# One-core hybrid encoder step: the triangular inverse and the gated scores on packed 32 by 32 tiles

## What is computed

```python
# gated delta rule, per chunk and head
M = where(strict, beta * rel * (k @ k.T), 0)
sol = triangular_solve(eye + M, rhs)            # the kernel forms the inverse itself
# HGRN2, per chunk and head
A[t, s] = sum_d q[t, d] * k[s, d] * exp(G[t, d] - G[s, d])   for s <= t
```

## Time and profile before

| | |
|---|---|
| runs, median (lowest to highest) | 1079.43 us (1077.76 to 1082.05), 3 runs |
| profiled execution, its own time | 1077.1 us |
| its span in the trace | 1075.3 us |
| PE busy, PEld busy | 1043.8 us, 1006.2 us |
| DVE busy, ACT busy | 506.8 us, 381.1 us |
| mean granted clock of TensorE | 0.995 of full |

### The profile page before, as it was taken

The page is one execution under the profiler, slowest core; times in us unless marked ns, Lnnn a source line. Parts: engine busy times, 40 slices in busy tenths (PEclk is TensorE's granted clock), DMA queues, the critical chain, the costliest instruction groups (busy, mean ns, idle before and its releaser), DMA issues.

```text
span 1075.3 us, 20690 instructions
## 1 busy us (share of the span) xinstructions
PE 1043.8 (97%) x8773; PEld 1006.2 (94%) x8773; DVE 506.8 (47%) x910; ACT 381.1 (35%) x663; POOL 17.3 (2%) x28
## 2 busy tenths in 40 slices
PE   6999999999999999999999999999999999999997
PEld 5888998899999999999999999999999999999996
DVE  3569435442224654744743475444444444343432
ACT  6675344523432234236333323232322232212222
POOL 0000000000001000000000000000000000000000
PEclk9999999999999999999999999999999999999999
DMA  9922223430333244243263323223233232322212
GB/s 325 275 62 60 60 79 79 108 86 2 99 83 111 79 109 127 75 118 99 89 172 88 100 79 92 86 78 88 87 88 88 78 97 79 89 84 80 88 55 84
DMA packets 181749, 104.95 MB, mean 98 GB/s; under 512 B 4578, under 2 KB 179144, under 8 KB 181676
## 3 DMA queue, kind: packets, MB, share of 16 engines
q1 hardware_dynamic: 179484, 96.74, 31.6%
q0 software_dynamic: 1568, 4.90, 1.6%
q10 hardware_dynamic: 624, 2.23, 0.6%
HBM read 100.55 MB, written 3.31 MB: 97 GB/s over the span
## 4 chain that ended last, share of the span: by engine, by line
PE 89%; DVE 3%; ACT 3%; SPq 3%; issue 1%; DMA 1%; ACTq 0%; DVEq 0%
PE G L1670 70%; PE R L1678 15%; PE R L1681 2%; SPq L783 2%; PE G L1708 1%; DVE cy L1369 1%; DMA raw<-in_w_in 1%; ACT Um L943 1%; ACT w_hi L906 0%; DVE w_lo L1210 0%; DVE kPG L1439 0%; ACT X L943 0%; DVE kD L1441 0%; SPq L785 0%; DVE relT L1412 0%
## 5 line engine op out<-in xcount | busy, mean ns | idle before, releaser
L1670 PE MATMUL G<-h_hi,w_hi 128*128 128x272 f32 (+1 forms) x1456 | 428.5, 294 | 1.0 <-DVE w_lo L1210 0.8
L1670 PE MATMUL G<-h_lo,w_hi 128*128 128x272 f32 (+1 forms) x1456 | 422.0, 290 | 0.0
L1670 PE MATMUL G<-h_hi,w_lo 128*128 128x272 f32 (+1 forms) x1456 | 421.6, 290 | 0.0
L1670 PEld LDWEIGHTS G<-h_hi,w_hi 128*128 128x128 f32 x1456 | 276.0, 190 | 3.2 <-issue 1.4
L1670 PEld LDWEIGHTS G<-h_lo,w_hi 128*128 128x128 f32 x1456 | 276.4, 190 | 0.0
L1670 PEld LDWEIGHTS G<-h_hi,w_lo 128*128 128x128 f32 x1456 | 276.0, 190 | 0.0
L1210 DVE TENSOR_TENSOR w_lo<-raw,w_hi 128x1024 fp32r<-128x1024 f32 (+2 forms) x138 | 158.4, 1147 | 244.8 <-ACT w_hi L906 244.6
L906 ACT ACTIVATE w_hi<-raw 128x1024 fp32r<-128x1024 f32 (+2 forms) x138 | 136.4, 988 | 104.4 <-PE G L1670 90.3
L1670 PE MATMUL G<-a_hi,w_hi 128*128 128x272 f32 (+2 forms) x340 | 98.4, 290 | 0.4 <-DVE w_lo L1210 0.4
L1670 PE MATMUL G<-a_hi,w_lo 128*128 128x272 f32 (+2 forms) x340 | 98.2, 289 | 0.0
L1670 PE MATMUL G<-a_lo,w_hi 128*128 128x272 f32 (+2 forms) x340 | 97.9, 288 | 0.0
(11 more groups left out here) (250 smaller groups left out, 1349.2 us busy)
## 6 DMA issues: line engine op xcount, KB each, us to landing
raw<-in_w_in SPq DMA_DIRECT2D x48, 512.0 KB, 5.9
raw<-in_w_up SPq DMA_DIRECT2D x44, 512.0 KB, 3.8
raw<-in_w_ada SPq DMA_DIRECT2D x32, 512.0 KB, 4.6
wada<-in_w_ada SPq DMA_DIRECT2D x8, 1024.0 KB, 11.1
raw<-in_w_down SPq DMA_DIRECT2D x16, 512.0 KB, 3.9
raw<-in_w_out SPq DMA_DIRECT2D x8, 512.0 KB, 4.0
raw<-in_w_down SPq DMA_DIRECT2D x8, 384.0 KB, 3.4
xtok<-in_x_prompt ACTq DMA_DIRECT2D x4, 512.0 KB, 5.7
```

What stands on the lines that cost most here:

```text
L1670: ins = pe.matmul(out, w, x, start=(job.first and k == 0 and p == 0), stop=(job.last and k == job.nk - 1 and p == 2))
```

## The change

What the diff does:

- **Inverse, levels 0 to 4.** Only 32 by 32 blocks on the diagonal matter there. T, its transpose and X live in packed tiles Tc, Uc, Xc of 128 partitions by 10 times 32 columns. A step of `g_x`, `g_t` or `g_y` is 34 products of 32 by 32: 4 chunks times 2 heads times 4 diagonal blocks, and 2 for the sample. Block j stands on partitions 32j to 32j+31 for operands and result. All 34 go into one fill of one bank. The transposes of `g_t` and of `g_x` at level 0 become products with the identity (`turned`).
- **Inverse, levels 5 and 6.** Level 5: `g_x` is 16 products of 32 by 32, `g_y` is two fills of 8 and 16 products. Level 6: 8 products of 64 by 64 each for `g_x` and `g_y`. `g_t` of level 5 goes away. The results are assembled in Um (block copies on ACT and DVE) and in T64.
- **Scores.** `h_diag` and `h_level` 0 to 4: 34 products that contract 128 channels into 32 by 32 results, result block j on partitions 32j to 32j+31; level 5: 16 such, level 6: 8 of 64 by 64. DVE copies under the mask into a packed tile Sc; after level 4 ACT copies its blocks to N or PT, and DVE copies the blocks of levels 5 and 6 there directly.
- **Reads.** Each level's result is read by one instruction of 128 partitions by 256 columns and one of 32 by 64.
- **Constants.** The masks on the chip shrink to 32 columns per level; POOL clears T64 and Um, the second after a wait for the evacuation of the group "gagb".
- **Plan.** NEED changes in four places, so that the jobs fall a little otherwise between the steps.

```diff
+PACK = 2 * N_CHUNK
+LAST_SMALL = 4
...
-    NEED = dict(g_gram=3.0, g_tok=4.0, g_x=0.9, g_y=0.9, g_t=0.2, g_w=1.0, g_u=1.2, g_o=1.6, h_diag=2.2, h_level=2.4, h_k=2.5,
+    NEED = dict(g_gram=3.0, g_tok=4.0, g_x=0.8, g_y=1.0, g_t=0.2, g_w=1.0, g_u=1.2, g_o=1.6, h_diag=2.2, h_level=2.4, h_k=2.5,
                 h_o=1.4, g_norm=0.6, onorm=0.4)
     def need(step):
         name = step[0]
         if name == "g_x" and step[2] == 0:
-            return 2.6
+            return 1.5
         if name == "g_y" and step[2] == LEVELS - 1:
-            return 3.4
+            return 1.6
...
+            if 0 < lv <= LAST_SMALL + 1:
+                s.append(("g_t", pair, lv - 1))
             if lv:
-                s.append(("g_t", pair, lv - 1))
                 s.append(("g_y", pair, lv))
...
-        "g_x": ["dve" if name == "g_x" and a[1] == 0 else "act"] * short,
-        "g_y": ["dve"] * short, "g_t": ["act"] * short,
+        "g_x": ["dve" if name == "g_x" and a[1] == 0 else "act"],
+        "g_y": ["dve", "act"] if name == "g_y" and a[1] == LAST_SMALL + 1 else ["dve"], "g_t": ["act"],
...
-        masks = sb("masks", [P, LEVELS + 1, P])
+        masks = sb("masks", [P, 1, P])
+        masks_c = sb("masks_c", [P, LAST_SMALL + 2, QUAD])
+        Sc = sb("Sc", [P, PACK + 2, QUAD])
...
-        Tm = at("rec", "Tm", [P, CHUNKS, 2, P], off=base + 2 * tile)
+        Tc = at("rec", "Tc", [P, PACK + 2, QUAD], off=base + 2 * tile)
+        Uc = at("rec", "Uc", [P, PACK + 2, QUAD], off=base + 2 * tile + (PACK + 2) * QUAD * 4)
+        T64 = at("rec", "T64", [P, PACK, P // 2], off=base + 2 * tile + 2 * (PACK + 2) * QUAD * 4)
         Um = at("rec", "Um", [P, CHUNKS, 2, P])
-        X = at("rec", "X", [P, CHUNKS, 2, P])
-        Wn = X
-        masks_t = at("rec", "masks_t", [P, LEVELS, P])
+        Wn = at("rec", "Wn", [P, CHUNKS, 2, P])
+        Xc = at("rec", "Xc", [P, PACK + 2, QUAD], off=where["rec"] - tile)
+        X5 = at("rec", "X5", [P, PACK, QUAD], off=where["rec"] - tile + (PACK + 2) * QUAD * 4)
+        X6 = at("rec", "X6", [P, PACK, P // 2], off=where["rec"] - tile + (2 * PACK + 2) * QUAD * 4)
+        masks_t = at("rec", "masks_t", [P, LAST_SMALL + 1, QUAD])
         cols_neg = at("rec", "cols_neg", [P, CHUNKS, NH])
...
+        def packed(b):
+            return R[:, b, 0:PACK * QUAD].rearrange("p (m t) -> p m t", m=PACK)
+        def packed_sample(b):
+            return R[0:DEC, b, PACK * QUAD:(PACK + 2) * QUAD].rearrange("p (h t) -> p h t", h=2)
+        def quad(j):
+            return slice(j * QUAD, (j + 1) * QUAD)
+        def block_of(x, r, c):
+            return x[quad(r), 0:N_CHUNK, :, quad(c)].rearrange("p c h t -> p (c h) t")
+        def corner_of(x):
+            return x[0:P // 2, 0:N_CHUNK, :, P // 2:P].rearrange("p c h t -> p (c h) t")
+        def corner(b):
+            return R[0:P // 2, b, 0:PACK * P // 2].rearrange("p (m t) -> p m t", m=PACK)
...
-            sp.dma_start(masks[:, 0:LEVELS, :], t["level_masks"][:, 0:LEVELS, :]).then_inc(const_in, 16)
+            sp.dma_start(masks_c[:, :, :], t["level_masks_c"]).then_inc(const_in, 16)
...
+                pool.dma_start(Tc[:, 0:PACK, :], mid(t["unit_c"], PACK)).then_inc(Tc_unit, 16)
+                pool.dma_start(Tc[0:DEC, PACK:PACK + 2, :], mid(t["unit_c"][0:DEC], 2)).then_inc(Tc_unit, 16)
...
+                    pool.memset(T64[0:P // 2, :, :], 0.0).then_inc(inverse_zero, 1)
+                    wait_group(pool, groups_at["gagb", 0])
+                    pool.memset(Um[:, :, :, :], 0.0).then_inc(inverse_zero, 1)
...
+            def read_packed(n, dst):
+                act.wait_ge(fill_done, first_fill[n] + 1)
+                b = first_fill[n] % 4
+                act.activation(dst[:, 0:PACK, :], packed(b), ACT.Copy)
+                act.activation(dst[0:DEC, PACK:PACK + 2, :], packed_sample(b), ACT.Copy).then_inc(bank_user["act"], 1)
...
-                elif name == "g_x" and a[1]:
-                    read_banks(n, 0, chunk_pieces(X, True)[:len(bank_users(step))])
+                elif name == "g_x" and 0 < a[1] <= LAST_SMALL:
+                    read_packed(n, Xc)
+                elif name == "g_x" and a[1] == LAST_SMALL + 1:
+                    read_banks(n, 0, [(X5[:, :, :], packed)])
+                elif name == "g_x" and a[1] == LEVELS - 1:
+                    read_banks(n, 0, [(X6[P // 2:P, :, :], lambda b: R[P // 2:P, b, 0:PACK * P // 2]
+                                       .rearrange("p (m t) -> p m t", m=PACK))])
                 elif name == "g_t":
-                    read_banks(n, 0, chunk_pieces(Um, True)[:len(bank_users(step))])
+                    read_packed(n, Uc)
+                    if a[1] == LAST_SMALL:
+                        act.wait_ge(inverse_zero, 2)
+                        wait_bank(act, first_fill[n])
+                        for j in range(4):
+                            act.activation(block_of(Um, j, j), Uc[quad(j), 0:PACK, :], ACT.Copy)
+                        act.activation(Um[0:DEC, N_CHUNK, :, 0:DEC], Uc[0:DEC, PACK:PACK + 2, :], ACT.Copy)
+                elif name == "g_y" and a[1] == LAST_SMALL + 1:
+                    act.wait_ge(fill_done, first_fill[n] + 2)
+                    b = (first_fill[n] + 1) % 4
+                    for r, c in ((0, 1), (2, 3)):
+                        ins = act.activation(block_of(Um, r, c), packed(b)[quad(r)], ACT.Copy)
+                    ins.then_inc(bank_user["act"], 1)
...
+                elif name == "h_level" and a[1] == LAST_SMALL:
+                    act.wait_ge(at_zero, a[0] + 1)
+                    wait_bank(act, first_fill[n])
+                    for j in range(4):
+                        act.activation(block_of(scores(a[0]), j, j), Sc[quad(j), 0:PACK, :], ACT.Copy)
+                    act.activation(scores(a[0])[0:DEC, N_CHUNK, :, 0:DEC], Sc[0:DEC, PACK:PACK + 2, :], ACT.Copy)
...
+            def copy_packed(n, dst, mask, lv):
+                b = bank(n, 0)
+                dve.copy_predicated(dst[:, 0:PACK, :], mid(mask[:, lv, :].bitcast(U32), PACK), packed(b))
+                read(dve.copy_predicated(dst[0:DEC, PACK:PACK + 2, :], mid(mask[0:DEC, lv, :].bitcast(U32), 2),
+                                         packed_sample(b)))
...
-                    if lv < LEVELS - 1:
-                        copy_masked(n, Tm, masks_t, lv)
+                    if lv <= LAST_SMALL:
+                        copy_packed(n, Tc, masks_t, lv)
+                        if lv == LAST_SMALL:
+                            dve.wait_ge(inverse_zero, 2)
+                            wait_bank(dve, first_fill[n])
+                            for j in range(2):
+                                dve.tensor_copy(T64[quad(j), :, quad(j)], Tc[quad(j), 0:PACK, :])
+                    elif lv == LAST_SMALL + 1:
+                        read(dve.tensor_copy(T64[quad(1), :, quad(0)], packed(bank(n, 0))[quad(1)]))
                     else:
-                        wait_bank(dve, last_bank[spot("g_t", pair, lv - 1)])
-                        copy_masked(n, Um, masks, lv)
+                        read(dve.tensor_copy(corner_of(Um), corner(bank(n, 0))))
...
+                    link(dve.memset(Sc[:, :, :], 0.0))
+                    copy_packed(n, Sc, masks_c, LAST_SMALL + 1)
...
+                    if lv <= LAST_SMALL:
+                        copy_packed(n, Sc, masks_c, lv)
+                    elif lv == LAST_SMALL + 1:
+                        b = bank(n, 0)
+                        for r, c in ((0, 1), (2, 3)):
+                            ins = dve.tensor_copy(block_of(scores(pair), r, c), packed(b)[quad(r)])
+                        read(ins)
+                    else:
+                        read(dve.tensor_copy(corner_of(scores(pair)), corner(bank(n, 0))))
...
+            def quads(lhsT, rhs):
+                return [mm(lambda b, m=2 * c + h, j=j: packed(b)[quad(j), m, :], lhsT(c, h, j), rhs(c, h, j))
+                        for c in range(N_CHUNK) for h in range(2) for j in range(4)] + \
+                       [mm(lambda b, h=h: packed_sample(b)[:, h, :], lhsT(N_CHUNK, h, 0), rhs(N_CHUNK, h, 0))
+                        for h in range(2)]
+            def turned(block):
+                return quads(block, lambda c, h, j: ident[quad(j), quad(j)])
...
+                    if lv == 0:
+                        for k in range(len(FILLS)):
+                            wait_bank(pe, first_fill[spot("g_gram", pair)] + k)
+                        fill(n, 0, turned(lambda c, h, j: N[quad(j), c, h, quad(j)]))
+                    elif lv <= LAST_SMALL:
+                        wait_bank(pe, first_fill[spot("g_y", pair, lv - 1) if lv > 1 else spot("g_x", pair, 0)])
+                        fill(n, 0, quads(lambda c, h, j: N[quad(j), c, h, quad(j)], lambda c, h, j: Tc[quad(j), 2 * c + h, :]))
+                    elif lv == LAST_SMALL + 1:
+                        wait_bank(pe, first_fill[spot("g_y", pair, LAST_SMALL)])
```

(63 more changed lines are left out.)

53 lines of the change are left out of this document (10 added, 43 removed).

## The result

The changed kernel takes 1062.9 us (median of 4 runs, 1060.2 to 1063.9) against 1079.05 for the kernel before in the same series: ratio 0.985, interval 0.983 to 0.987. It is faster by 16 us; 39 were forecast. The side is right and the time lies in the range, but more than half of the expected gain is missing.

The account below looks back on a forecast made before the run. PE was taken to bound the kernel. Inverse -31.8, scores -18.6, new waits +9.1, DVE's score waits +2 and masks -0.6 summed to -39.9 us, so 1040 us was forecast, range 1029 to 1086.

Parts of the forecast that it names:

- What bounds the kernel: Whole kernel: PE, busy 97% of the span; other engines matter only where PE would wait for them.
- The price of a packed product: Inverse and scores: 0.008 us a record on four fully overlapping tiles, so a packed step takes 0.78 us against 2.02.
- New waits +9.1: Inverse: single-fill steps leave PE standing about 0.8 us at twelve bare places, adding 9.1 us.
- The clock: After stretches with waits the granted clock may fall again, as once to 0.94 for 28 us, costing 1.7 us.
- The sign of being wrong: On PE: a piece of 68 records above 1.6 us, or waits above 25 us in sum.
- Scores -16.6: Scores stage: packed products save 18.6 us, less 2 us of new waits on DVE.
- it fits on average: Scores, pair 1: two levels need 6.6 us of DVE against 8.0 of PE; late levels were put at +2.
- Masks at the start -0.6: Kernel start: smaller mask loads (896 KB become 176) let weights land earlier, saving 0.6 us.
- Half overlap: Packed products: loads and products each need their own slot, 0.014 us a record, +15.4 us: 1055; chance 0.18.
- Waits twice as long, or PE's clock: Bare places cost 1.6 us, +11: 1051, or the clock falls; beyond the main case, up to 1070, chance 0.06.
- Issue-bound: Packed products: PE cannot feed short records faster than 0.026 us each, giving 1085; chance 0.17.
- Only the scores overlap: Inverse: blocks on different array rows serialise at 0.032 us a record, +45 us, giving 1085; chance 0.09.

Follow-up runs that it names:

- burst: The changed kernel plus two bursts of 512 unread 32 by 32 products on four diagonal tiles: 1130.2 us, ratio 1.049 to the kernel before.
- dve_turn: The changed kernel with the levels' block transposes made by DVE, not by 34 identity products on PE: 1032.9 us, ratio 0.958 to the kernel before.
- scores_only: The kernel before with only the gated scores packed, the inverse left as it was: 1067.2 us, ratio 0.990 to the kernel before.

## Why the prediction was half right

- **What bounds the kernel**: right. PE was it and still is (95% busy).
- **The price of a packed product**: right for a step, wrong for a run of steps. The step took 0.76 us for 0.78, at 0.65 without the entry, and alike in inverse and scores. Level 6 came as priced too, 1.07 us for 1.1. The failed step is the sentence that took 0.008 because "the array sets the pace, not the issue": it priced the 34 products by the time they hold the array, and put no price on their being 136 instructions in place of 40 (in `g_t`, of 20). In the sum, a term for PE's code is missing; it measured 12.2 us of halts.

  Per level `g_x`, `g_t`, `g_y` and half a job are 3 x 136 + 48 = 456 instructions. At 3.73 us for 256 their code takes 6.6 us (my estimate, from `burst`); the array needs 3 x 0.76 + 3.2, with a bare wait of 0.6, 6.1. So even such a level uses up code about as fast as it arrives. In pair 0 there is twice only an adaLN pair of 1 us where the half job should be, and then 472 instructions meet 3.9 us of array time. The longest halt follows the first of these: from 117.75 us to its end at 127.78 PE ran 728 instructions in 10.0 us, and at the burst's pace they take 10.6. The next 507 took 11.3 us, more than the burst's pace gives; why is open.

  In pair 1 the levels took 6.9, 7.2 and 8.6 us from `g_y` to `g_y`. The 6.9 had no halt and is what its steps and its two bare waits cost (0.76 + 3.22 + 1.45 + 1.46); the 8.6 had two short halts. In `dve_turn` a level has 320 instructions, 4.7 us of code, and takes 5.4 to 5.8 in pair 1.
- **New waits +9.1**: right, 8.4, with the twelve places of 0.8 from start to start.
- **The clock**: nothing in the sum, and in the forecast only a small rival (1.7 us in the row). It took about 11 us: the second missing term. The halts alone don't explain it. 20.5 of the 37.5 us at the lower level lie at halts, but `dve_turn` with 2.5 us of halts still has 23.9 us there, and `scores_only` with none 13.7. Executions of one kernel differ in it as well: the kernel before ran from 1075.9 us at a mean clock of 0.995 to 1081.9 at 0.989. What draws the rest, the waits or the packed steps themselves, stays open.
- **The sign of being wrong**: the forecast named waits of PE above 25 us in sum. PE's idle time is 28.1 us between 94 and 338 us alone, and 57.6 in the whole run, before 31.5.
- **Scores -16.6**: -13.4. The products are as priced. DVE's waits were put at +2, and PE's idle time of 338 to 500 us rose by 4.8. The term that was mis-sized is this one, and the argument behind it is "it fits on average": one meeting with the low part of a weight tile costs 2.2 us, as the timeline of ACT and DVE shows ahead of PE's longest wait there.

```profile
437.43 1.06 ACT L930 ACTIVATE w_hi<-raw 128x1024 fp32r<-128x1024 f32 x1 [7.78 <-DMA raw<-in_w_in]
438.52 1.23 DVE L1264 TENSOR_TENSOR w_lo<-raw,w_hi 128x1024 fp32r<-128x1024 f32 x1 [4.41 <-ACT w_hi L930]
439.66 0.43 DVE L1306 COPY_PREDICATED Sc<-masks_c,R 128x256 f32<-128x256 uint32 x1
...
441.92 0.99 PE L1744 MATMUL R<-inp 128*32 128x32 f32 x32 [2.21 <-DVE inp L1581]
```

  The weights land late, ACT's high part is late, and DVE takes the low part first: the masked copy stands behind it and the whole chain with it. The 1.7 us at 475 us are of the same kind: the low part of a weight tile starts at 472.60, the square of `o` at 473.74, and only then comes the update of S for which PE waits.
- **Masks at the start -0.6**: -0.5, right.
- **Half overlap** (1055) came nearest to the time, for a wrong reason: no step takes its 1.2 us at the full clock.
- **Waits twice as long, or PE's clock** (1051, to 1070 beyond that): the waits were as long as forecast. Its other half, the clock, came true and is about half of what is missing in the inverse.
- **Issue-bound** (1085): half true. A limit beside the array exists, 0.029 us a record against its 0.026, but it holds over hundreds of instructions, not for each record, and jobs of long products let PE catch up. Hence a part of its loss and not all. The Trainium skill ("TensorE: Matmul & The Clock Gate", the part on the 56 ns gap) says that starts are never under about 25 ns apart. The trace does not agree: 68 records started within 0.65 us, 0.0096 apiece.
- **Only the scores overlap** (1085): fell. The inverse's steps take 0.76, the scores' 0.77. The Trainium skill ("TensorEngine Tiling (Array Packing)", Gotcha 1: PSUM Pressure) says that different row tiles cannot access one PSUM bank at the same time. The trace does not agree: the 0.76 us are of steps whose four blocks write one bank, on partitions of their own.

## What to carry to other kernels

Cutting a product into small packed ones saves array time but multiplies instructions; count them beside the array's time, over a whole level and not over one step, and fill the rest with long products or give the cheap ones (block transposes) to another engine. Here 1360 instructions fewer were worth 30 us, though the products among them had taken only 7.6 us of the array. Idle time with no releaser in the middle of a step, at a fixed distance in instructions, is the mark of it in a profile.
